# Three attention stages rewritten as one program: transposed value product in groups of four query tiles, with PE doing it ahead of the transposes

## The reference, cut to what matters

```python
# neighbourhood attention (once): 8 x 16 window on a 16 x 64 grid, learned bias, gated by silu(z)
s = einsum('qd,kd->qk', q, k) * d ** -0.5 + bias;  s = where(valid, s, NEG)
y = einsum('qk,kd->qd', softmax(s), v) * silu(z)
# dilated attention (once in each of two layers): slope_h * |pos_q - pos_k|, three dilation patterns mixed
s = einsum('qd,kd->qk', q, k) * d ** -0.5 - slope[h] * abs(pos_q - pos_k) + log(multiplicity)
# latent attention (once in each layer): 64 + 32 columns for q and k, no bias
s = (einsum('qd,kd->qk', q_nope, k_nope) + einsum('qr,kr->qk', q_rot, k_rot)) * 96 ** -0.5
y = einsum('qk,kd->qd', softmax(s), v)
```

## Time and profile before

| | us |
|---|---|
| median of three runs (lowest, highest) | 4722.94 (4722.29, 4726.23) |
| the profiled execution: its time, its span | 4719.33, 4717.5 |
| busy in the span: PE 87%, DVE 47%, POOL 37%, ACT 32% | 4091.2, 2223.5, 1734.4, 1502.9 |
| mean granted clock of TensorE | 0.944 of full speed |

### The profile page before, as it was taken

The page is one execution under the profiler, slowest core; times in us unless marked ns, Lnnn a source line. Parts: engine busy times, 40 slices in busy tenths (PEclk is TensorE's granted clock), DMA queues, the critical chain, the costliest instruction groups (busy, mean ns, idle before and its releaser), DMA issues.

```text
span 4717.5 us, 60741 instructions
## 1 busy us (share of the span) xinstructions
PE 4091.2 (87%) x22152; PEld 3489.1 (74%) x22152; DVE 2223.5 (47%) x4269; ACT 1502.9 (32%) x2417; POOL 1734.4 (37%) x1140
## 2 busy tenths in 40 slices
PE   2999665888689798997899999698998995999998
PEld 1888555777578687886688888576887884888887
DVE  2443585532466565553444443465665543233323
ACT  2221233431233674441211221333773432222221
POOL 2433123531354462002444444453660013444442
PEclk8999888999899899998999999799999997999999
DMA  6665332631135422222123221245323221111111
GB/s 156 195 176 154 100 89 64 137 99 49 72 94 139 105 72 53 48 71 82 63 85 107 77 98 32 85 112 147 79 55 68 48 92 40 41 54 50 49 45 50
DMA packets 300704, 404.65 MB, mean 86 GB/s; under 512 B 45908, under 2 KB 224980, under 8 KB 299860
## 3 DMA queue, kind: packets, MB, share of 16 engines
q1 hardware_dynamic: 293496, 375.60, 28.5%
q10 hardware_dynamic: 6912, 25.17, 1.9%
HBM read 316.23 MB, written 93.63 MB: 87 GB/s over the span
## 4 chain that ended last, share of the span: by engine, by line
PE 67%; issue 8%; DVE 7%; POOL 5%; ACT 3%; DMA 3%; DVEq 2%; SPq 2%; POOLq 1%; ACTq 0%
PE ps L849 10%; PE ps L449 6%; PE ps L450 5%; PE ps L451 5%; PE ps L839 5%; PE ps L1788 5%; PE ps L1789 5%; PE ps L1790 5%; PE ps L1804 5%; PE ps L1806 4%; PE ps L1805 4%; POOL rs L738 2%; PE ps L885 1%; PE ps L886 1%; PE ps L1475 1%
## 5 line engine op out<-in xcount | busy, mean ns | idle before, releaser
L404 POOL TENSOR_TENSOR WL<-RAW,WH 128x1024 fp32r<-128x1024 f32 x226 | 556.2, 2473 | 1194.9 <-ACT WH L386 1184.6
L449 PE MATMUL ps<-WH,XTh 128*128 128x512 f32 (+1 forms) x1536 | 611.6, 398 | 47.7 <-POOL XTl L498 25.1
L451 PE MATMUL ps<-WL,XTh 128*128 128x512 f32 (+1 forms) x1536 | 601.0, 391 | 0.0
L450 PE MATMUL ps<-WH,XTl 128*128 128x512 f32 (+1 forms) x1536 | 600.9, 391 | 0.0
L386 ACT ACTIVATE WH<-RAW 128x1024 fp32r<-128x1024 f32 x226 | 234.5, 1063 | 826.1 <-PE ps L1806 347.7
L1824 DVE TENSOR_TENSOR X<-ps,X 128x512 f32<-128x512 f32 x512 | 349.1, 689 | 254.1 <-PE ps L1806 253.1
L1788 PE MATMUL ps<-XTh,WH 128*128 128x512 f32 x1024 | 401.7, 392 | 18.4 <-POOL XTl L498 18.4
L1804 PE MATMUL ps<-WH,Hh 128*128 128x512 f32 x1024 | 401.2, 392 | 4.0 <-DVE X L1824 3.3
L1789 PE MATMUL ps<-XTl,WH 128*128 128x512 f32 x1024 | 400.6, 391 | 0.0
L1790 PE MATMUL ps<-XTh,WL 128*128 128x512 f32 x1024 | 400.4, 391 | 0.0
L1805 PE MATMUL ps<-WH,Hl 128*128 128x512 f32 x1024 | 398.7, 389 | 0.0
(11 more groups left out here) (196 smaller groups left out, 7680.5 us busy)
## 6 DMA issues: line engine op xcount, KB each, us to landing
RAW<-w_all SPq DMA_DIRECT2D x232, 512.0 KB, 3.7
WM<-w_mod ACTq DMA_DIRECT2D x48, 512.0 KB, 4.3
WM<-w_mod SPq DMA_DIRECT2D x48, 512.0 KB, 4.1
QS<-QA_d SPq DMA_DIRECT2D x24, 512.0 KB, 3.8
KHs<-KA_d SPq DMA_DIRECT2D x48, 256.0 KB, 6.1
KLs<-KA_d SPq DMA_DIRECT2D x48, 256.0 KB, 6.8
VS<-VA_d SPq DMA_DIRECT2D x20, 512.0 KB, 7.2
X<-x SPq DMA_DIRECT2D x2, 4096.0 KB, 13.9
```

What stands on the lines that cost most here:

```text
L404: e.tensor_tensor(w_low(n), w_raw(n), w_high(n).bitcast(F32), ALU.subtract).then_inc(w_ready, 1)
L449: e.matmul(bank, a, w, start=(kc == 0), stop=False)
L450: e.matmul(bank, b, w, start=False, stop=False)
L451: j = e.matmul(bank, a, l, start=False, stop=(kc == K - 1))
```

## The change

`softmax_pv_pe`, `biased_body` and `out_loop` are gone. A class `Heads` and one function for each engine serve na, dil and mla. For a group G of four query tiles of one head, the transposed exponentials are kept as a high and a low part (`PTh`, `PTl`, each up to 8 tiles of keys by 512 queries); V is split in high and low columns side by side (`VHL`), and the product has V as the stationary operand and 512 columns of queries. The result `[value column, query]` is copied to SBUF (`OT`) and turned back by four small float32 products with `twoI` (two identities on top of each other, which also adds the two halves). The core of the diff, new lines:

```diff
+            def turn(u):                                   # PE
+                n = len(a.tiles(u % T))
+                e.wait_ge(s["exp"], a.u0 + u + 1)
+                for b in range(2):
+                    ge(e, s["lo"], 2 * (a.u0 + u) - 1 + b)
+                    for k in range(4 * b, min(4 * b + 4, n)):
+                        j = e.transpose(ps[:, 4 + b, (k % 4) * P:(k % 4) * P + P], a.P[:, u % 2, k * P:k * P + P], ident[:])
+                    j.then_inc(s["tr"], 1)
+            def values(G, part):
+                h, g = divmod(G, 2)
+                keys = a.group(g)                           # 8 tiles of keys, 6 for na
+                if part == 0:
+                    e.wait_ge(s["lo"], 8 * (a.g0 + G + 1))
+                    e.wait_ge(s["vlo"], a.h0 + h + 1)
+                    ge(e, s["ot_copied"], a.g0 + G)
+                third = (len(keys) + 2) // 3
+                for n in range(third * part, min(third * part + third, len(keys))):
+                    v = a.VHL[:, h % 2, keys[n], :]
+                    e.matmul(ps[:, 6, :], v, a.PTh[:, G % 2, n, :], start=(n == 0), stop=False)
+                    j = e.matmul(ps[:, 6, :], v, a.PTl[:, G % 2, n, :], start=False, stop=(n == len(keys) - 1))
+                if part == 2:
+                    j.then_inc(s["ot"], 1)
+            def turn_back(G):
+                e.wait_ge(s["ot_copied"], a.g0 + G + 1)
+                ge(e, s["out"], a.g0 + G)
+                for r in range(4):
+                    j = e.matmul(ps[:, 7, 64 * r:64 * r + 64], a.OT[:, G % 2, r * P:r * P + P], twoI[:], start=True, stop=True)
+                j.then_inc(s["back"], 1)
+            scores(0)
+            for u in range(N_UNITS + 4):
+                G, r = divmod(u, 4)
+                if u + 1 < N_UNITS:
+                    scores(u + 1)
+                if G >= 1 and r < 3:
+                    values(G - 1, r)
+                if G >= 1 and r == 3:
+                    turn_back(G - 1)
+                if u < N_UNITS:
+                    turn(u)
...
+            def high(u):                                   # ACT; r = u % 4, G = u // 4
+                for b in range(2):
+                    e.wait_ge(s["tr"], 2 * (a.u0 + u) + 1 + b)
+                    e.activation(a.PTh[:, G % 2, n0 + k0:n0 + k1, r * P:r * P + P],
+                                 ps[:, 4 + b, 0:(k1 - k0) * P].rearrange("p (k q) -> p k q", q=P), ACT.Copy).then_inc(s["hi"], 1)
+            value_high(0)
+            if a.kind == "dil":
+                distances(0)
+            exps(0)
+            for u in range(N_UNITS + 4):
+                G, r = divmod(u, 4)
+                if u + 1 < N_UNITS:
+                    exps(u + 1)                             # waits for max of u + 1
+                if a.kind == "dil" and u % 2 == 0 and u + 2 < N_UNITS:
+                    distances(u + 2)                        # DIST times slope, 1024 wide
+                if G >= 1 and r == 3:
+                    copy_out(G - 1)                         # waits "ot"; ps bank 6 -> OT; then_inc "ot_copied"
+                if u < N_UNITS:
+                    high(u)
+                if u % T == 5 and u + 3 < N_UNITS:
+                    value_high(u // T + 1)
...
+            maxes(0)                                       # DVE
+            for u in range(N_UNITS + 5):
+                G, r = divmod(u, 4)
+                if u + 1 < N_UNITS:
+                    maxes(u + 1)                            # waits "full", "bias"; writes the negated maximum
+                if u < N_UNITS:
+                    low(u)                                  # two subtractions ps - PTh -> PTl, each waits "hi"; then_inc "lo"
+                if G >= 2 and r == 0:
+                    output(G - 2)                           # reciprocal, drain, 256-wide product (na: drain and a second one)
...
+                c0 = (T - 1 - t) * P                       # POOL, far(u), dil
+                if u % 2 == 0:
+                    e.wait_ge(s["dist"], a.own // 2 + u // 2 + 1)
+                else:
+                    e.tensor_scalar(BId[:, 1, :], DIST[:, t, :], SL[:, h:h + 1], None, ALU.mult)
+                    e.drain()
+                e.tensor_tensor(BId[:, u % 2, :], BId[:, u % 2, :], TB[:, c0:c0 + S], ALU.add).then_inc(s["bias"], 1)
...
+            value_low(0)
+            for u in range(N_UNITS):
+                if a.kind != "mla":
+                    far(u)
+                if u % T == 7 and u + 1 < N_UNITS:
+                    value_low(u // T + 1)                   # waits "vhi"; 512 wide
```

More of the change, by code:

```diff
@@ L127, in shape_tables @@
         "row_mask": rmask.reshape(P, 3 * NA_KEYS), "inv_freq": np.tile(inv, (P, 1)),
-        "slopes": np.tile(np.array([-(2.0 ** (-8.0 * (h + 1) / H_DIL)) for h in range(H_DIL)], np.float32)[:, None, None], (1, P, 1)),
+        "slopes": np.tile(np.array([[-(2.0 ** (-8.0 * (h + 1) / H_DIL)) for h in range(H_DIL)]], np.float32), (P, 1)),
         "eps_sums": np.tile(np.array([Q_LORA * EPS, KV_LORA * EPS, ROPE * EPS] + [NOPE * EPS] * 4 + [ROPE * EPS] * 4, np.float32), (P, 1)),
@@ L162, in build_program @@
         mhalf = sb("mhalf", [P, 16])
+        twoI = sb("twoI", [P, 64])
         GT = sb("GT", [P, D])
@@ L318, in build_program @@
         PJ = {n: sems(n, proj_names) for n in ("pj1", "pj2")}
[L319 to L325, removed]
+        diff_loop = sems("diff", "used full max exp tr pta ptb pv out comb sq rs")
+        heads_all = sems("heads", "full max exp tr hi lo vhi vlo ot ot_copied back out")
+        loads = "ld0 ld1 vld0 vld1 pos"
+        AT = {"diff": {**diff_loop, **sems("diff", "ld0 ld1")}, "na": {**heads_all, **sems("na", loads + " bias")},
+              "dil": {**heads_all, **sems("dil", loads + " bias dist dists posf")}, "mla": {**heads_all, **sems("mla", loads)}}
         out_names = sems("out", "full upd")
@@ L819, in c @@
                 return self.units + k + CREDIT
[L821 to L862, removed]
         def copy_turned(who, a, u, ptbuf, ktiles, half):
@@ L1311, in dil_attention @@
                 e.tensor_scalar(rs1[:], rs1[:], -1.0, None, ALU.mult)
-                e.drain().then_inc(s["dist"], 1)
+                e.drain().then_inc(s["posf"], 1)
+                e.wait_ge(s["dists"], L + 1)
             if key == "act":
-                e.wait_ge(s["dist"], L + 1)
+                e.wait_ge(s["posf"], L + 1)
                 for t in range(T):
-                    e.activation(DIST[:, t, :], POSF, ACT.Abs, bias=rs1[:, t:t + 1])
+                    j = e.activation(DIST[:, t, :], Sd[:, 0, :], ACT.Abs, bias=rs1[:, t:t + 1])
@@ L1317, in dil_attention @@
+                j.then_inc(s["dists"], 1)
                 e.drain()
             if key == "pool":
[L1319 to L1415 removed]
@@ L1449, in mla_attention @@
+                e.wait_ge(s["dists"], L + 1)
+            heads(who, Heads("dil", L, 1 + 2 * L))
         def mla_attention(who, L):
@@ L1505, in out_product @@
+            heads(who, Heads("mla", L, 2 + 2 * L))
         def out_product(who, s, L, first, gated):
```

419 lines of the change are left out of this document (226 added, 193 removed).

## The result

The changed kernel takes 5353.35 us (median of 4 runs, 5346.86 to 5357.43), against 4723.24 (median of 4, 4722.29 to 4726.23) for the kernel before: ratio 1.1332, 95% interval [1.1312, 1.1351]. It is slower by 630 us. The prediction was 5275, with a range of 5160 to 5400 and a chance of 0.96 on slower.

What follows compares the result with a forecast made beforehand. PE was taken to bound dil and mla before the change, a ring of waits over DVE and ACT after it. Dil 320, mla 132, na 72.5 and 17, small parts 14: 556 us on 4719.3 gives 5275, range 5160 to 5400.

Steps and rivals of the forecast that it cites:

- The ring: Waits over DVE and ACT (max, next exponential, high, low): 4.41 us a unit in dil, 4.29 mla, 3.29 na.
- rival 4: PE stays the bound and the kernel gets faster: 4475 us, chance 0.03.
- Dil's even step: Dil's second ring, every other unit, over exponential, distances, POOL's addition and maximum: 6.36 us.
- Dil's odd step: Dil's other units: POOL's scaling taken as hidden in the ring, so 4.41 us.
- The group's extra: Last unit of each group: transposes wait for turning back and ACT's copy; 3.7 us in dil, 2.95 in mla and na.
- rival 2: PE at low clock becomes a bound: 38 us more per mla stage, 15 per dil, 20 in na; 5400, chance 0.17.
- the signs by which the prediction would have called itself wrong: Maxima waiting for PE's scores, ACT's high before the next unit's exponential, or dil under 5 us a unit.
- the output: DVE work once per group between low and max: 0.57 us in mla, 1.0 in na, hidden in dil.
- The extra of 2.4 at each of na's heads: Na's bias at each head ready 9.0 us after a maximum began, ring wants 6.6: 7 heads, +17 us.
- The tails: End of each stage: a whole group's product, copy and turning back, +3.2 us, five times, +16.
- Rival 1: Clock stays full, 2.2 us per group everywhere: 5193 us, chance 0.20.
- Rival 3: PE's order costs nothing, a group pays 0.5 us: 5060 us, chance 0.09.

Runs made afterwards that it cites:

- e6: Changed kernel with the turning back a unit later and all dil distances scaled on ACT ahead of the exponentials: 4973.86 us.
- e5: e6 with ACT's copy of the result and high(u) also ahead of the next unit's exponential: 4657.69 us, ratio 0.9867 to the kernel before.
- e3: Changed kernel with ACT's next exponential moved behind the distances, the copy of the result and high(u): 4796.07 us.
- e8: e5 with PE's transposes directly behind the next unit's scores, values and turning back behind them: 4635.64 us, ratio 0.983 to the kernel before.
- e4: Changed kernel with dil's distances ahead of the exponentials in ACT's order, still shared with POOL: 5207.28 us.
- e7: Changed kernel with the turning back a unit later in PE's order, behind the next unit's scores: 5112.7 us.
- e1: Changed kernel with the turning back behind the unit's transposes in PE's order instead of in front: 5263.84 us.

## Why the prediction was right, and where its terms were off

**The ring** was the main step, and it held. Forecast 4.29 a unit in mla and 3.29 in na; measured 4.18 and 3.13. In mla the difference is in high to low and the low behind it, put at 0.71 + 1.20 and measured 0.62 + 1.21, and in hops of 0.02. That the ring rests on high(u) standing behind exp(u+1) is shown by e6 and e5, which differ in that order: 316 us. In e3 it gives 557 together with much of the other two waits. That is also the condition that rival 4 named ("if high(u) did not stand behind exp(u+1)"), and with the other two waits removed the kernel is indeed faster than before. Its 4475 was too low: it put PE's unit at 2.95 us in dil and 3.4 in mla as the bound, where e8, its nearest form, has 220.2 / 63 = 3.50 in dil, where ACT with all distances is busy 95%, and 222.2 / 63 = 3.53 in mla.

**Dil's even step** was forecast 6.36 and measured 6.2, by the path it named; e4 shows it by removing it.

**Dil's odd step** failed. The term was POOL's scaling, bounded between 0 and "at most another addition of 2.33" and taken as hidden below 1.9, on the ground that it reads one input where the addition reads two. It measures 2.84, longer than the addition's 2.36. The prediction's own formula then works: the odd bias comes x + 2.5 = 5.34 behind the even maximum, and the step is 5.33, not 4.41. It adds the 0.9 to one unit of four, as the prediction had said it would for a long scaling, some 15 us for each dil stage. The timeline of e7, which has nothing else on this step, shows the whole of it: 2.84, a gap of 0.14, 2.36 and the maximum 0.14 behind.

```profile
1701.08 2.84 POOL L1533 TENSOR_SCALAR BId<-DIST,SL 128x1024 f32<-128x1024 f32 x1
1701.22 1.22 DVE L1463 CUSTOM_DVE_ANT_0 Sd<-ps,BId 128x1024 f32<-128x1024 f32 x1 [0.28 <-POOL BId L1535]
...
1704.06 2.36 POOL L1535 TENSOR_TENSOR BId<-BId,TB 128x1024 f32<-128x1024 f32 x1
1706.56 1.23 DVE L1463 CUSTOM_DVE_ANT_0 Sd<-ps,BId 128x1024 f32<-128x1024 f32 x1 [0.99 <-issue]
```

The Trainium skill (GPSIMD Engine Reference, 3.1 Elementwise) gives a best case of 1.8 cycles an element for a tight loop, by which the prediction estimated 1.5 us, and explains the slower rate of the addition by its two inputs. For this instruction, with one scalar per partition, the trace disagrees by almost a factor of two, and the measurement decides.

**The group's extra** was 3.7 in dil and, as a mean over two clocks, 2.95 in mla and na. In the trace the clock is at the lower of its two levels whenever PE turns back between the first and the last maximum of a stage: 1.97 for the eight products in all 70 cases, behind idle times of 4.1 to 8.6. At full clock the same eight take 1.10, as in the second row here, from na's tail, where PE was idle only 0.69 before; the first has 2.12 before it (timeline of the changed kernel):

```profile
1089.71 1.97 PE L1376 MATMUL ps<-twoI,OTn 128*128 128x64 f32 x8 [2.12 <-ACT OTn L1425]
...
1099.38 1.10 PE L1376 MATMUL ps<-twoI,OTn 128*128 128x64 f32 x8 [0.69 <-ACT OTn L1425]
```

So the mean over two levels was the wrong choice for mla and na: 3.7 was nearer. By the Trainium skill (TensorE: Matmul & The Clock Gate, HAM oscillation) all three stages would pay 3.7; the trace agrees, with 1.97 each time. On top come in mla the scores, which stand behind turning back and transposes in PE's order: 0.70 on the row at 2241.74, from 0.10 to 1.24 and 0.84 in the mean of the 14 last steps of the first mla stage. Then 4.29 + 3.7 + 0.84 = 8.83; measured are 8.12 to 9.27, in the mean 8.87 (8.73 is the median). The prediction had listed who waits for the turning back and left out the second follower; rival 2 had named late scores, but as a cost of each unit. The plain units do not pay it (4.18 at a mean clock of 0.83). Maxima that wait for scores were also one of the signs by which the prediction would have called itself wrong, and 8.73 lies above the 6.5 to 8.0 that it gave for this step. In this one step the sign did appear; it does not touch the ring, where no plain maximum waits for scores.

The prediction also counted 15.75 groups per stage, but only 14 turnings back lie between the first and the last maximum. The steps of a stage, summed by their place in a group, show what held and what cancelled:

| stage | last of a group: forecast, measured | first | second | third |
|---|---|---|---|---|
| first dil | 127.7, 127.5 | 100.2, 99.7 | 69.5, 85.3 | 100.2, 92.9 |
| first mla | 114.0, 130.9 | 76.5, 77.0 | 67.6, 66.9 | 67.6, 62.7 |
| na, heads in the third | 98.3, 97.6 | 67.6, 75.0 | 51.8, 50.1 | 68.8, 64.1 |

In dil the +15.8 is POOL's scaling, and half of it is hidden by the even steps, which were shorter and in the third place 15, not 15.75. The last steps come out even only because 14 steps of 8.35 in the mean and two short ones stand where 15.75 of 8.11 were forecast. In mla +16.9 is the clock and the scores, against -5.6 from the shorter ring and the count. Na's 286.7 against 286.6 is luck: the ring was 10 too high, while the first steps, forecast with 1.0 for the output, took 7.4 more than forecast. What holds them was not tried in this kernel. The extra of 2.4 at each of na's heads is in the trace as forecast (5.58 against 3.13, seven times).

**The tails** failed most for their size: 14 forecast, 47 found, of which 46 lie behind the last maxima: 8.9 in na, 9.9 and 8.6 in dil (8.5 became 18.4 and 17.2), 9.4 both times in mla (8.5 became 17.8). The term was "one group's product, copy and turning back against one unit's work, +3.2", at full clock and alone. Na's last maximum is followed by 15.0 us of work (1086.71 to 1101.70), against 6.1 before (996.12 to 1002.25), so +8.9. In it are two turnings back instead of none, the transposes and lows of the last unit behind the first of them, and twelve value products of which most run at the lower clock: 1094.14 to 1098.73, 4.6 us. Nothing hides these, as no other work of the stage is left.

The sum closes: dil +15.6, mla +23.3, na +0.1 and the tails +33 are 72, and 5346.86 - 5275 = 71.9. The time is inside the range and the ring within 5% of its forecast; what the forecast was low by is the tails, mla's last step and POOL's scaling.

**The rivals.** Rival 1 (clock stays full) is contradicted by 1.97 at each turning back between the maxima. Rival 2 (PE at the low clock a bound) is contradicted by the plain steps, and its late scores are there in mla's last step. Rival 3 (PE's order costs nothing) is contradicted by e7, where 241 us go with it.

## What to carry to other kernels

When two engines with a fixed order feed each other more than once per unit, write down the chain from one instruction back to itself through both orders; its length is a floor of the unit, however idle the engines are, and moving one call can open it (557 of 630 us here, and 316 us where the other two waits were already gone). A wait put into an engine's order delays everything issued behind it until that engine is level again, so list all its followers, the next unit's first operation too. After a ring is opened, read the busy shares again before the next reordering: in mla of e5 PE was busy 214 of 222 us, and e8's new order had nothing to win there.

## What the runs showed of the hardware that was not expected

- POOL's product with one scalar per partition, 128x1024 float32, takes 2844 ns (64 of them), longer than its addition of two tensors of that shape, 2360 ns (128).
- The turning back ran at the lower clock after idle times of 2.12 us in na's tail and at the full one after 2.22 us in e3's dil, and in e1's na at the lower one after 1.01, so the idle time in front of it alone does not tell the level. The row of e3 (timeline):

```profile
1707.61 1.10 PE L1376 MATMUL ps<-twoI,OTd 128*128 128x64 f32 x8 [2.22 <-ACT OTd L1425]
```

What decides between the two was not tried.
